# A two-block stack on one core: conv and pooling projections with 512 moving columns, part of the weight split moved to GpSimd

## The chip, the cores and the metric

The kernel runs on one core of a Trainium2 chip. The metric is the device time of one execution in microseconds. Before the change it is 1310.85 us, the median of three runs (1310.82 to 1310.9).

## The reference, cut to what matters

256 tokens of width 1024 go through two layers of a first block and one layer of a second. The change touches the first block, of which this is the part:

```
h = rms_norm(x, g_mix)
b_a, c_a, x_a, u_p, q, k, v, ga, gp, gt = split(h @ w_in)
y_a = (b_a * depthwise_conv3(c_a * x_a, conv_w)) @ w_a_out
y_p = pooled(u_p) by groups of 256 channels, windows 2, 4, 8, 16, each minus u_p,
      @ w_pool per group, * pool_scale
y_t = windowed_gqa(q, k, v, rel_bias, sink) @ w_attn_out
merged = sigmoid(ga) * y_a + sigmoid(gp) * y_p + sigmoid(gt) * y_t
x = x + merged @ w_o
h2 = rms_norm(x, g_ffn);  x = x + swiglu(h2 @ w_gu) @ w_down
```

## The kernel before, in words

Every float32 operand of a projection is held as a rounded high part and a low part (the rest), and a product is made of three matmuls: high weights by high and by low activations, and low weights by high activations. Both parts of the activations h lie beside each other in `h`.

The weights come as a stream of chunks of 128 x 2048 (`STREAM`), 1 MB each. SyncE loads them into a ring of four slots (line 640), and reloads a slot when the semaphore `wl_ready` says that its low part has been made. ScalarE makes the high part of a chunk in two halves (`split_high`, line 1571), VectorE the low part, `ring - high`, in two halves (`split_low`, line 2170); the halves are 128x1024. There are two split buffers, so the high part of a chunk waits until the chunk two before it has been used by TensorE (`BEFORE`, `NEXT`). `next_high` and `next_low`, called in the handling of a job, split the chunk two ahead.

TensorE works through a fixed list of jobs, `LAYER_JOBS`, one chunk each: v, k, four q, two kd, then four rounds of c, x, b (conv gate c, conv input x, conv gate b), then ga/wa, four u (pooling inputs), gp, wp, gt, wt, wo, and the feed-forward. A job makes 256 output columns, two groups of 128, for 256 tokens. `project` (x, b, u) puts both groups into one PSUM bank, 256 columns each, and multiplies the high weights by the two parts of h in two matmuls of 256 columns (line 788), 32 in all, then the low weights in 16 (line 794). `project_both` (q, c, gate, up) multiplies the high weights by both parts in one matmul of 512 columns (line 808), 16 in all, which leaves the main product and the cross part side by side in two banks; then the low weights, 16 of 256 columns (line 814). Its result needs ScalarE to copy the cross part out of PSUM and VectorE to add the main part. c, x and b use banks 0 and 1, 2, and 3.

Attention is laid between these jobs. After a job in `ATT_EARLY` (b0, c1, b1, c2, b2, c3, b3, ga0 and on; in layer 1 also c0) TensorE turns the probabilities of two steps ago (line 1029) and makes the scores of a step (line 1017), for which VectorE must have read the scores before (`s_read`). VectorE runs `softmax_out` of the step before at the start of such a job's handling (lines 2286 to 2290) and `softmax_in` at its end (lines 2276 to 2281); ScalarE makes the exponentials between them (line 1656).

VectorE handles the jobs in order. c: sum into `stage`. x: `stage * x` into `upad` (line 2332), then three taps of the convolution for two groups (lines 2339 and 2157). b: product with the convolution into `tmp` (line 2347), low part of the next chunk, low part of `feed`. u: the window sums (line 2359), edges, difference and the low part of `feed`.

GpSimd issues DMAs: the attention bias in four groups of eight (line 667), rows, and the 48 transfers of the second block's modulation weights (line 702), each behind a wait. It also clears a few tiles and makes one tensor_tensor, over 128x8, in the second block (line 722).

## Time and profile before

| what | value |
|---|---|
| runs | 1310.85 us median (1310.82 to 1310.9) |
| the profiled execution | 1310.87 us, its span 1309.1 us |
| TensorE (PE) busy | 1293.9 us, 99% of the span |
| VectorE (DVE) busy | 1043.4 us, 80% |
| ScalarE (ACT) busy | 715.8 us, 55% |
| GpSimd (POOL) busy | 57.1 us, 4% |
| DMA | 262.64 MB, mean 201 GB/s |

The page gives busy times as shares of the span. The chain of waits goes back from the last instruction to what released it, step by step, and says on which engine the time of the chain was spent. The groups of instructions give, for each source line, the busy time, the mean time of one in ns, and the idle time of the engine just before them with what ended it. The first layer's conv rounds run from about 50 to 118.5 us, its pooling inputs from 173.6 to 196.7 us; the second layer's conv rounds from about 520 to 596 us.

### The profile page before, as it was taken

How to read it: one execution, taken by the hardware profiler on the slowest of the kernel's cores; microseconds unless marked ns; L12 is line 12 of the kernel's file. 1: busy time of each engine (PE TensorE's matmuls, PEld its weight loads, DVE VectorE, ACT ScalarE, POOL GpSimd, SP SyncE). 2: the span in 40 equal slices, each digit the busy share in tenths (PEclk: the TensorE clock that was granted, in tenths of full speed). 3: DMA queues.
4: the chain of work that ended last, by engine and by line, in shares of the span. 5: the costliest groups of instructions: out<-in, count | busy, mean ns of one | idle time of the engine just before them, and what ended most of it. 6: DMA issues, size and time to landing. Idle time of an engine off the chain costs nothing.

```text
span 1309.1 us, 19856 instructions
## 1 busy us (share of the span) xinstructions
PE 1293.9 (99%) x7564; PEld 1122.8 (86%) x7564; DVE 1043.4 (80%) x1730; ACT 715.8 (55%) x1149; POOL 57.1 (4%) x108
## 2 busy tenths in 40 slices
PE   8999999999999999999999999999999999999998
PEld 7999898888888888998898888888879887888887
DVE  4887677877778786977687777788888898798888
ACT  5655655455454455555545464454477566655554
POOL 1111000000000000000000000000010000000000
PEclk9999999999999999999999999999999999999999
DMA  8865545764777745454446755878635515255551
GB/s 292 270 212 185 177 161 212 250 232 150 271 258 284 253 165 193 161 181 153 149 162 229 274 181 216 271 280 290 236 111 176 212 66 171 103 203 187 193 192 64
DMA packets 43000, 262.64 MB, mean 201 GB/s; under 512 B 5645, under 2 KB 6413, under 8 KB 15646
## 3 DMA queue, kind: packets, MB, share of 16 engines
q1 hardware_dynamic: 32688, 227.28, 48.9%
q0 software_dynamic: 10128, 34.06, 8.2%
q8 instruction: 60, 0.98, 0.3%
q14 instruction: 30, 0.25, 0.1%
q10 hardware_dynamic: 94, 0.07, 0.0%
HBM read 259.81 MB, written 1.58 MB: 200 GB/s over the span
## 4 chain that ended last, share of the span: by engine, by line
PE 94%; DVE 3%; ACT 1%; DMA 0%; issue 0%; SPq 0%; POOL 0%; DVEq 0%; POOLq 0%; ACTq 0%
PE psum L808 21%; PE psum L855 17%; PE psum L929 12%; PE psum L814 11%; PE psum L862 9%; PE psum L788 8%; PE psum L794 4%; PE psum L1017 1%; PE psum L1040 1%; PE psum L1203 1%; PE psum L1029 1%; PE psum L947 1%; DVE split L2164 1%; DMA ring<-stream 0%; PE psum L745 0%; PE psum L826 0%
## 5 line engine op out<-in xcount | busy, mean ns | idle before, releaser
L2164 DVE TENSOR_TENSOR split<-ring,split 128x1024 fp32r<-128x1024 f32 x406 | 479.3, 1219 | 59.7 <-ACT split L1571 58.4
L1571 ACT CAST split<-ring 128x1024 fp32r<-128x1024 f32 x405 | 405.7, 1050 | 174.8 <-PE psum L929 68.2
L808 PE MATMUL psum<-h,split 128*128 128x512 f32 x1216 | 290.0, 390 | 0.0
L808 PEld LDWEIGHTS psum<-h,split 128*128 128x128 f32 x1216 | 225.0, 188 | 44.7
L929 PE MATMUL psum<-split,feed 128*128 128x512 f32 x792 | 185.2, 390 | 0.0
L929 PEld LDWEIGHTS psum<-split,feed 128*128 128x128 f32 x792 | 146.8, 188 | 29.4 <-DVE split L2164 0.2
L814 PEld LDWEIGHTS psum<-h,split 128*128 128x128 f32 x1216 | 156.2, 191 | 6.1
L814 PE MATMUL psum<-h,split 128*128 128x256 f32 x1216 | 158.0, 283 | 0.0
L855 PE MATMUL psum<-split,h 128*128 128x512 f32 x632 | 155.8, 393 | 0.1
L855 PEld LDWEIGHTS psum<-split,h 128*128 128x128 f32 x632 | 116.3, 188 | 23.6 <-issue 0.4
L788 PE MATMUL psum<-h,split 128*128 128x256 f32 x896 | 112.2, 283 | 0.0
L788 PEld LDWEIGHTS psum<-h,split 128*128 128x128 f32 x896 | 109.7, 192 | 0.2
L1691 ACT COPY arena<-psum 128x512 f32<-128x512 f32 x40 | 23.4, 586 | 114.4 <-PE psum L814 114.4
L862 PE MATMUL psum<-split,h 128*128 128x512 f32 x316 | 81.7, 390 | 0.0
L855 PE MATMUL psum<-split,feed 128*128 128x512 f32 x304 | 74.8, 392 | 0.3 <-DVE feed L2164 0.3
L862 PEld LDWEIGHTS psum<-split,h 128*128 128x128 f32 x316 | 59.3, 188 | 12.5
L1656 ACT ACTIVATE arena<-arena,small 128x256 f32<-128x256 f32 x64 | 32.1, 502 | 69.3 <-DVE small L2281 69.3
L855 PEld LDWEIGHTS psum<-split,feed 128*128 128x128 f32 x304 | 56.0, 188 | 11.7 <-DVE feed L2164 0.6
L794 PE MATMUL psum<-h,split 128*128 128x256 f32 x448 | 58.5, 283 | 0.0
L2492 DVE SCALAR_TENSOR_TENSOR arena<-arena 128x1024 f32<-128x1024 f32 x48 | 58.5, 1218 | 0.0
L794 PEld LDWEIGHTS psum<-h,split 128*128 128x128 f32 x448 | 55.9, 192 | 0.0
L2157 DVE SCALAR_TENSOR_TENSOR arena<-arena,prm 128x255 f32<-128x255 f32 (+2 forms) x120 | 52.6, 480 | 3.8 <-ACT arena L2139 2.3
(378 smaller groups left out, 1365.0 us busy)
## 6 DMA issues: line engine op xcount, KB each, us to landing
ring<-stream SPq DMA_DIRECT2D x213, 1024.0 KB, 4.9
arena<-ada POOLq DMA_DIRECT2D x48, 512.0 KB, 5.8
arena<-bias_by_distance POOLq DMA_DIRECT2D x32, 96.0 KB, 5.2
gain<-norm_rows POOLq DMA_DIRECT2D x4, 512.0 KB, 6.0
x<-x_in SPq DMA_DIRECT2D x2, 512.0 KB, 4.1
ring<-stream SPq DMA_DIRECT2D x2, 512.0 KB, 6.9
arena<-norm_rows POOLq DMA_DIRECT2D x2, 512.0 KB, 5.7
gain<-mod_rows POOLq DMA_DIRECT2D x2, 512.0 KB, 6.0
```

What stands on the lines that cost most here:

```text
L788: pe.matmul(to[m], w[0][:, at + k, cols[m]], rhs[:, part, at + k, :], start=m == parts[0] and k + part == 0, stop=False)
L794: mm = pe.matmul(to[m], w[1][:, at + k, cols[m]], rhs[:, 0, at + k, :], start=False, stop=m == parts[-1] and k == kts - 1)
L808: pe.matmul(bank[b + m].rearrange("p (a t) -> p a t", a=2), w[0][:, k, m * P:(m + 1) * P], h[:, :, k, :], start=k == 0, stop=False)
L814: mm = pe.matmul(bank[b + m][:, T:2 * T], w[1][:, k, m * P:(m + 1) * P], h[:, 0, k, :], start=False, stop=k == KT - 1)
L855: pe.matmul(bank[banks[i]], lhs[:, part, k0 + k, at], w[0][:, k, :], start=k0 + k + part == 0, stop=False)
L862: mm = pe.matmul(bank[banks[i]], lhs[:, 0, k0 + k, at], w[1][:, k, :], start=False, stop=k0 + k == KT - 1)
L929: mm = pe.matmul(bank[4 + 2 * i + n], feed[:, part, place, at], w[which][:, k, cols], start=j + k + part + which == 0, stop=last and j == ...
L1571: act.copy(split_of(x)[:, 0, n], ring[:, AT[x] % RING, n]).then_inc(wh_ready, 1)
L1656: act.activation(S1[:, i % 2, hh, :], S1[:, i % 2, hh, :], ACT.Exp, scale=-1.0, bias=nm[:, i % 2, hh:hh + 1], accum_out=rs[:, i % 2, hh:hh ...
L2157: return dve.scalar_tensor_tensor(out_, a, s, b, op0, op1)
L2164: return dve.tensor_tensor(out_, value, high.bitcast(F32), ALU.subtract)
L2492: dve.scalar_tensor_tensor(w, w, 0.5, c_row, ALU.mult, ALU.mult, accum_out=mod_l[:, a:a + 1]) \
```

## The change

x, b and u jobs are made by `project_both` as well: 16 matmuls of 512 columns in place of 32 of 256. Each of these jobs then leaves a cross part. ScalarE copies it (into `tmp` for x, `stage` for b, `padded` for u) and VectorE adds the main part before it goes on as before. The three conv jobs use two pairs of banks in turn (0 and 1, 2 and 3), and so do the u jobs; a job waits until the sum of the job two before it is made (`wide_summed`). For 14 chunks a layer (b0, c, x and b of rounds 1 to 3, u0 to u3) GpSimd makes the second half of the low part; VectorE makes the first, and waits before the first half of the following chunk until GpSimd's is counted, so that `wl_ready` goes up in order. In GpSimd's queue three of these stand between bias groups 1 and 2 (the wait for x1's job is gone), seven between groups 2 and 3, four behind the loads for the second block, and in layer 1 all 14 ahead of the modulation transfer 24.

The diff, cut to its core:

```diff
+POOL_LOWS = ([("b", 0)] + [(n, j) for j in (1, 2, 3) for n in ("c", "x", "b")] + [("u", j) for j in range(4)])
...
+        def summed(l, name, j):
+            return wide_summed, l * 16 + (12 + j if name == "u" else 3 * j + "cxb".index(name)) + 1
+
+        def conv_bank(name, j):
+            return ({"c": 0, "x": 2, "b": 0}, {"c": 2, "x": 0, "b": 2})[j % 2][name]
...
+            def second_low(x):
+                n = slice(CHUNK // 2, CHUNK)
+                pool.wait_ge(wh_ready, AT[x] * 2 + 2)
+                pool.wait_ge(wl_ready, AT[x] * 2 + 1)
+                pool.tensor_tensor(split_of(x)[:, 1, n], ring[:, AT[x] % RING, n], split_of(x)[:, 0, n].bitcast(F32), ALU.subtract) \
+                    .then_inc(wl_ready, 1)
...
             bias_group(1)
-            pool.wait_ge(job_done, JOB["x", 1])
+            for x_ in POOL_LOWS[0:3]:
+                second_low((0, *x_))
             bias_group(2)
+            for x_ in POOL_LOWS[3:10]:
+                second_low((0, *x_))
             pool.wait_ge(job_done, JOB["b", 3])
             bias_group(3)
...
+            for x_ in POOL_LOWS[10:]:
+                second_low((0, *x_))
...
+                if a == ADA_L:
+                    for x_ in POOL_LOWS:
+                        second_low((1, *x_))
...
TensorE's waits and jobs:
+                    elif (name, j) == ("x", 0):
+                        pe.wait_ge(*release(("kd", 1), l))
+                    elif name == "x":
+                        pe.wait_ge(*summed(l, "b", j - 1))
+                    elif name == "b":
+                        pe.wait_ge(*summed(l, "c", j))
+                    elif name == "u" and j < 2:
+                        pe.wait_ge(*release((("ga", 3), ("wa", 3))[j], l))
+                    elif name == "u":
+                        pe.wait_ge(*summed(l, "u", j - 2))
...
-                    elif name in ("x", "b"):
-                        mm = project(CONV_BANK[name], c, h)
+                    elif name in ("c", "x", "b"):
+                        mm = project_both(conv_bank(name, j), c)
...
+                    elif name == "u":
+                        mm = project_both(2 * (j % 2), c)
...
ScalarE:
+                    elif name == "x":
+                        act.wait_ge(job_done, l * NJOBS + k + 1)
+                        if j >= 1:
+                            act.wait_ge(yin_ready, l * 4 + j)
+                        act.copy(tmp, cross_part(conv_bank(name, j))).then_inc(wide_cross, 1)
+                    elif name == "b":
+                        act.wait_ge(job_done, l * NJOBS + k + 1)
+                        act.wait_ge(dve_evac, l * len(DVE_JOBS) + dve_count(("x", j)))
+                        act.copy(stage, cross_part(conv_bank(name, j))).then_inc(wide_cross, 1)
...
-                        act.copy(padded[:, :, PADW:PADW + T], src).then_inc(act_evac, 1)
+                        act.copy(padded[:, :, PADW:PADW + T], cross_part(2 * (j % 2))).then_inc(act_evac, 1)
...
VectorE:
             def split_low(x, half_=None):
                 for half in range(2) if half_ is None else (half_,):
+                    if half and x[0] < L and x[1:] in POOL_LOWS:
+                        continue
+                    before = STREAM[AT[x] - 1]
+                    if half == 0 and before[0] < L and before[1:] in POOL_LOWS:
+                        dve.wait_ge(wl_ready, AT[x] * 2)
...
+                        dve.wait_ge(*summed(l, "c", j))
+                        dve.wait_ge(wide_cross, l * 8 + 2 * j + 1)
+                        dve.tensor_tensor(tmp, main_part(conv_bank(name, j)), tmp, ALU.add).then_inc(wide_summed, 1)
+                        dve.wait_ge(*summed(l, "x", j))
+                        dve.tensor_tensor(upad[:, :, 1:1 + T], tmp, stage, ALU.mult).then_inc(dve_evac, 1)
...
+                        dve.wait_ge(wide_cross, l * 8 + 2 * j + 2)
+                        dve.tensor_tensor(stage, main_part(conv_bank(name, j)), stage, ALU.add).then_inc(wide_summed, 1)
+                        dve.wait_ge(*summed(l, "b", j))
+                        dve.tensor_tensor(tmp, stage, y1, ALU.mult).then_inc(dve_evac, 1)
...
+                        u_ = padded[:, :, PADW:PADW + T]
+                        dve.tensor_tensor(u_, main_part(2 * (j % 2)), u_, ALU.add).then_inc(wide_summed, 1)
+                        dve.wait_ge(*summed(l, "u", j))
```

## Rows read from the trace of the kernel before

**Rows 1.** The page: busy time by engine; the granted clock; the chain by engine.

```profile
PE 1293.9 (99%) x7564; PEld 1122.8 (86%) x7564; DVE 1043.4 (80%) x1730; ACT 715.8 (55%) x1149; POOL 57.1 (4%) x108
PEclk9999999999999999999999999999999999999999
PE 94%; DVE 3%; ACT 1%; DMA 0%; issue 0%; SPq 0%; POOL 0%; DVEq 0%; POOLq 0%; ACTq 0%
```

**Rows 2.** Waits of PE, the longest in total: total us, times, longest us.

```profile
PE psum L826 <- DVE h L2164: 1.8, 3, 0.9
```

**Rows 3.** Busy time by stretch: a conv round of layer 0, the u jobs.

```profile
core 0: us, PE busy (x) PEld busy (x) DVE busy (x) ACT busy (x) POOL busy (x), PEclk, DMA share, GB/s
81.50:100.40 18.90, 18.90 (x146) 18.23 (x145) 16.50 (x40) 10.21 (x21) 0.00 (x0) 1.00 0.47 167
173.60:196.70 23.10, 23.10 (x194) 23.07 (x193) 18.73 (x33) 11.30 (x14) 0.00 (x0) 1.00 0.47 170
```

**Rows 4.** Timeline of PE, conv jobs of both layers: start us, duration us.

```profile
69.10 4.00 PE L788 MATMUL psum<-h,split 128*128 128x256 f32 x32
72.94 2.08 PE L794 MATMUL psum<-h,split 128*128 128x256 f32 x16
...
557.20 3.83 PE L808 MATMUL psum<-h,split 128*128 128x512 f32 x16
560.87 2.08 PE L814 MATMUL psum<-h,split 128*128 128x256 f32 x16
```

**Rows 5.** Groups by line of PE: busy us, mean ns | idle before.

```profile
L808 PE MATMUL psum<-h,split 128*128 128x512 f32 x1216 | 290.0, 390 | 0.0
L788 PE MATMUL psum<-h,split 128*128 128x256 f32 x896 | 112.2, 283 | 0.0
```

**Rows 6.** Groups by line: the copy of ACT, the sum of DVE.

```profile
L1731 ACT COPY arena<-psum 128x512 f32<-128x512 f32 x8 | 4.7, 587 | 17.0 <-PE psum L794 17.0
L2328 DVE TENSOR_TENSOR arena<-psum,arena 128x512 f32<-128x512 f32 x8 | 5.5, 685 | 0.4 <-ACT arena L1729 0.4
```

**Rows 7.** Groups by line of POOL: all its tensor work.

```profile
L709 POOL MEMSET arena<- 128x1024 f32 x3 | 2.7, 954 | 13.6 <-PE psum L862 13.6
L722 POOL TENSOR_TENSOR arena<-arena 128x8 f32<-128x8 f32 x1 | 1.7, 1673 | 88.4 <-DVE arena L2850 88.4
L719 POOL MEMSET arena<- 128x8 f32 x1 | 0.1, 124 | 0.0
```

**Rows 8.** DVE beside POOL's memsets: timeline, and the cast line's min/median/max.

```profile
961.36 1.51 POOL L706 MEMSET arena<- 128x512 f32 x4 [22.63 <-DVE x L2157]
962.58 0.57 DVE L2572 CAST h<-arena 128x512 fp32r<-128x512 f32 x1
...
976.50 2.74 POOL L709 MEMSET arena<- 128x1024 f32 x3 [13.62 <-PE psum L862]
976.52 2.36 DVE L2164 TENSOR_TENSOR split<-ring,split 128x1024 fp32r<-128x1024 f32 x2
...
L2572 DVE CAST h<-arena x8: 420/427/574, 959.5 to 1125.5; 128x512 fp32r<-128x512 f32 x8
```

**Rows 9.** Timeline behind a b job of layer 0, PE and DVE.

```profile
97.18 2.36 DVE L2164 TENSOR_TENSOR split<-ring,split 128x1024 fp32r<-128x1024 f32 x2
100.44 3.83 PE L808 MATMUL psum<-h,split 128*128 128x512 f32 x16
104.26 0.48 DVE L2276 CUSTOM_DVE_ANT_0 arena<-psum,arena,minus_sinks 128x256 f32<-128x256 f32 x1
106.19 0.16 DVE L2286 TENSOR_TENSOR small<-small 128x2 f32<-128x2 f32 x1 [1.25 <-ACT small L1658]
106.38 0.72 PE L1017 MATMUL psum<-k_pair,q_first 128*128 128x256 f32 x4
112.89 0.69 DVE L2332 TENSOR_TENSOR arena<-psum,arena 128x512 f32<-128x512 f32 x1 [1.72 <-PE psum L794]
```

**Rows 10.** Timeline of POOL: a group of bias DMAs.

```profile
69.08 4.15 POOL L667 DMA_DIRECT2D arena<-bias_by_distance  x8 [19.09 <-PE psum L814]
```

More of the change, by code:

```diff
@@ L465, in bass_stack_kernel @@
         feed_high = sem("feed_high")
-        c_summed = sem("c_summed")
+        wide_summed = sem("wide_summed")
+        wide_cross = sem("wide_cross")
         ao_split = sem("ao_split")
@@ L1057, in _ @@
                         if (name, j) == ("ga", 0):
-                            pe.wait_ge(c_summed, l * 4 + 4)
+                            pe.wait_ge(*summed(l, "x", 3))
+                        elif name == "gp" and j % 2 == 0:
+                            pe.wait_ge(*summed(l, "u", 2 + j // 2))
                         elif j % 2 == 0:
@@ L1074, in _ @@
                         else:
-                            pe.wait_ge(c_summed, l * 4 + j)
-                    elif name in ("x", "b"):
-                        pe.wait_ge(*release((name, j - 1) if j else ("kd", CONV_BANK[name] - 2), l))
+                            pe.wait_ge(*summed(l, "x", j - 1))
+                    elif (name, j) == ("x", 0):
[8 more added lines that the diff above has]
+                        pe.wait_ge(*summed(l, "u", j - 2))
                     elif k >= 4 and name != "wo" and LAYER_JOBS[k - 4][0] != "wo":
@@ L1727, in _ @@
                         if j >= 1:
-                            act.wait_ge(dve_evac, l * len(DVE_JOBS) + dve_count(("x", j - 1)))
-                        act.copy(stage, cross_part(CONV_BANK[name])).then_inc(act_evac, 1)
+                            act.wait_ge(dve_evac, l * len(DVE_JOBS) + dve_count(("b", j - 1)))
+                        act.copy(stage, cross_part(conv_bank(name, j))).then_inc(act_evac, 1)
+                    elif name == "x":
[7 more added lines that the diff above has]
+                        act.copy(stage, cross_part(conv_bank(name, j))).then_inc(wide_cross, 1)
                     elif name == "u":
-                        act.copy(padded[:, :, PADW:PADW + T], src).then_inc(act_evac, 1)
+                        act.copy(padded[:, :, PADW:PADW + T], cross_part(2 * (j % 2))).then_inc(act_evac, 1)
                     if name == "wo" and j == 1:
@@ L2327, in _ @@
                         dve.wait_ge(act_evac, l * len(ACT_JOBS) + act_count(("c", j)))
-                        dve.tensor_tensor(stage, main_part(CONV_BANK[name]), stage, ALU.add).then_inc(c_summed, 1)
+                        dve.tensor_tensor(stage, main_part(conv_bank(name, j)), stage, ALU.add).then_inc(wide_summed, 1)
                     if name == "x":
-                        dve.wait_ge(c_summed, l * 4 + j + 1)
-                        dve.tensor_tensor(upad[:, :, 1:1 + T], halves(CONV_BANK[name]), stage, ALU.mult).then_inc(dve_evac, 1)
+                        dve.wait_ge(*summed(l, "c", j))
[3 more added lines that the diff above has]
+                        dve.tensor_tensor(upad[:, :, 1:1 + T], tmp, stage, ALU.mult).then_inc(dve_evac, 1)
                         dve.wait_ge(dve_evac, l * len(DVE_JOBS) + dve_count(("x", j)))
@@ L2346, in _ @@
                             dve.wait_ge(yin_ready, l * 4 + j)
-                        dve.tensor_tensor(tmp, halves(CONV_BANK[name]), y1, ALU.mult).then_inc(dve_evac, 1)
+                        dve.wait_ge(wide_cross, l * 8 + 2 * j + 2)
+                        dve.tensor_tensor(stage, main_part(conv_bank(name, j)), stage, ALU.add).then_inc(wide_summed, 1)
+                        dve.wait_ge(*summed(l, "b", j))
+                        dve.tensor_tensor(tmp, stage, y1, ALU.mult).then_inc(dve_evac, 1)
                         next_low((l, name, j))
```

4 lines of the change are left out of this document (removed).

## The prediction, made before the run

> **What bounds the kernel now.** I read the page first. TensorE is busy 1293.9 of 1309.1 us and carries 94% of the chain of waits, and the granted clock is full, level 2.4 GHz, in every slice; VectorE is busy 80%, ScalarE 55%, GpSimd 4% [rows 1]. Then TensorE's own waits: the longest in total is 1.8 us, three times, and belongs to none of the conv or pooling-input jobs [rows 2]. So TensorE's issue sets the time, and a change can gain only by fewer or cheaper matmuls. It can lose much more, by making TensorE wait. The second question is therefore how near VectorE is to the bound in the stretch that changes. In one round of three conv jobs (c, x, b) TensorE needs 18.9 us and VectorE is busy 16.5; in the four pooling-input jobs it is 18.7 of 23.1 [rows 3]. A round leaves VectorE only 2.4 us.
>
> The profiled execution took 1310.87 us, 1.77 beyond its span of 1309.1; the median is 1310.85, so the sum needs no correction.
>
> **The gain: wide matmuls.** Per job, 32 matmuls of 256 columns (high weights by both parts of h) become 16 of 512; the 16 low ones stay. In the timeline 32 narrow ones take 3.84 us up to the first low one (69.10 to 72.94), 16 wide ones 3.67 (557.20 to 560.87) [rows 4]: 0.17 us a job. The whole-run groups give 32 x 112.2/896 = 4.01 against 16 x 290.0/1216 = 3.82, or 0.19 [rows 5]. I take 0.175. x, b and u are 12 jobs a layer, 24 in all: 24 x 0.175 = 4.2 us, bounds 4.1 and 4.6. TensorE is the bound here, so all of it counts if nobody else becomes late. The weight loads halve too, which hides behind the columns.
>
> **ScalarE.** x and b now each need a copy of the cross part, 0.586 us; u had its copy already, of the same size [rows 6]. That is 8 x 0.59 = 4.7 us a layer on an engine busy about 10 us of a round's 18.9 [rows 3]. I cost its busy time at nothing, but not its order: x's copy stands behind the previous step's exponentials, and VectorE's sum for x waits for it.
>
> **VectorE, added and removed.** Added: 12 sums a layer from PSUM, 0.69 us each [rows 6], 2 to a round: +1.4. Removed: the second low half of 14 chunks, 1.18 us each (two take 2.36) [rows 8], 3 to a round: -3.5. So VectorE's own round falls from 16.5 to 14.4, under TensorE's new 18.9 - 2 x 0.175 = 18.55. If this were all, the change would be a clean gain.
>
> **GpSimd's halves: their length.** No row has a GpSimd subtraction of this size. From below: its memset of 128x1024 takes 0.95 us, one of 128x8 0.12, so one stream of 1024 costs 0.83 above a fixed 0.12; the instruction must also read two tiles. From above: its one tensor_tensor, a power over 128x8, took 1.67 us; with three streams of 0.83 behind that, 4.2 [rows 7]. Two input streams taken in turn give 1.8, all three in turn 2.6: I take 2.2. The Trainium skill, GPSIMD Engine Reference, section 3.1, measures 4497 ns for 2048 elements, by which this would be an estimate of 2.25 us; no run shows it yet.
>
> Is TensorE late for them? Each is needed when the job reaches its fifth low matmul, 3.67 + 0.48 = 4.15 us into the job, and the first half was ready before the job began in this trace's rounds (low of c's chunk 97.2 to 99.5, c begins 100.44) [rows 9]. VectorE's next first half also waits for it, about 3.3 us later. At 2.2 us neither waits; from about 5 us TensorE would.
>
> **GpSimd beside VectorE.** This decides the sign. Before, GpSimd never reads tiles while VectorE does. What the trace has: two lows of VectorE beside three memsets took 2.36 us, not slowed at all; but a VectorE cast beside a memset took 574 ns where its median is 427 [rows 8]. So the two engines do hinder each other in some pairings, and the new one, both reading two SBUF tiles, is not among those shown. Bounds: nothing, or the whole 2.2 us of each half during which every VectorE instruction with two SBUF inputs stands still. I take the whole for those instructions: reading is what both do most here, and the one pairing that was hindered shows that access is not free. The Trainium skill, SBUF — State Buffer, section "Who interferes with whom", states this outright: a VectorE instruction with two SBUF inputs contends with a GpSimd one that reads SBUF, not with one that only writes, and whoever comes second blocks for the whole instruction. Its second half agrees with the undisturbed lows of [rows 8]; the first no row shows.
>
> Now the round, at full taking of turns. Three halves are 3 x 2.2 = 6.6 us. Beside two of them VectorE can do the score instructions, which read PSUM, two of 0.48 us a step [rows 9]: 1.9 overlap, 4.7 left. 14.4 + 4.7 = 19.1. Two idle times don't go away: softmax_out waits 1.25 us for ScalarE's exponentials where steps follow each other [rows 9], and x's sum now waits for ScalarE's copy behind the exponentials (copy, 0.59, and part of the 1.7 us that VectorE idled for TensorE there before): I count 1.0. Together 21.35 against 18.55: VectorE is 2.8 us a round late. With a hold of h in place of 2.2 this is 3h - 3.8.
>
> Where it lands, by the round whose c job begins at 100.44: softmax_out, sum, product, first low and feed low follow. GpSimd's half (started by the first low of the c chunk) holds 2.2 of it, the sum adds 0.69, the missing half gives back 1.18. The second score instruction began at 104.26 and TensorE asked for it at 106.38 [rows 9], so a first delay of 1.7 is covered. In the next rounds it is TensorE's scores (the wait on s_read) that are late, and behind them x's job; the chunk lows of c come 1 us late too. Attention steps run in every round, so nothing recovers before ga. The rounds concerned are about three a layer (b of round 0 to b of round 3): 6 x 2.8 = 16.8, less the 1.7 of cover in each layer, 3.4: 13.4 us lost. In the pooling stage VectorE's round gives 4 x 0.69 more and four halves elsewhere; it has 4.4 us free, and four gate jobs with little VectorE work follow: at most 0.5 a layer, counted 0.
>
> Sum: -4.2 + 13.4 = +9.2, 1310.85 + 9.2 = 1320.
>
> **Other moved things, cost nothing.** Bank waits: x, b, c now wait for the sum two jobs back, 1.3 to 2 us after that job, with a job of 5.6 between. Later low halves delay a ring slot's reload by 2 us: a chunk is loaded about three jobs (17 us) ahead. GpSimd's queue: the 8 bias DMAs of 4.15 us each group [rows 10] now stand behind or between the lows; the next low is needed some 8 us later, and the heads they bring only at step 8. In layer 1 the lows stand ahead of an ada transfer that waited for the last pooling job anyway.
>
> **Rivals.**
> A, no hindrance: GpSimd works truly beside VectorE. For it: undisturbed lows beside memsets. Against: those only write. VectorE keeps 14.4 + 2.3 of waits = 16.7 under 18.55, TensorE never waits: 1310.85 - 4.2 = 1306.7.
> B, partial: the halves fall into VectorE's idle time more than I count, or are shorter. A hold of 1.7 us loses 3 x 1.7 - 3.8 = 1.3 a round, 7.8 in six, less 3.4 of cover is 4.4, which eats the gain: 1311.
> C, a GpSimd half takes 4.2 us or more, the bound from above: 3 x 4.2 - 3.8 = 8.8 a round, 52.8 in six, less 3.4 and the gain of 4.2 is +45: 1356, and from about 5 us TensorE waits for the halves themselves.
> The other side of the forecast is A; it decides from the point where the hold is under 1.7 us, for then the round's loss no longer pays for the gain.
>
> **Chances.** Forecast 0.52 (own range 1314.5 to 1333: holds of 1.9 us, 11.4 - 3.4 - 4.2 = +3.8, to 2.6, 24.0 - 3.4 - 4.2 = +16.4, and 6 more if the cover is less and the pooling stage pays too), A 0.35, B 0.09, C 0.04. A measurement tells 0.2%, 2.6 us, from no change. Faster: A and a hold so small that gain remains, 0.36. Same 0.10. Slower 0.54. The range goes from under A, 1305.8, to 1333.
>
> **What would show it.** Gain right: the groups of 256-column high matmuls of x, b, u gone, 384 more wide ones, 3.66 us from first wide to first low. Hold right: during each GpSimd subtraction no VectorE instruction with two SBUF inputs is under way (or it is stretched to its end), TensorE waits for VectorE before the score matmuls and the c jobs, and a round takes over 20 us. A right: rounds of 18.5 us and VectorE idle over 3 us in each. Wrong altogether: loss in the pooling stage, or waits on bank sums.

## The result and the profile after

The changed kernel takes 1333.86 us (median; 1332.51 to 1334.18) beside 1310.88 us for the kernel before on the same chip: a ratio of 1.0173, 95% interval 1.016 to 1.0186, or 23.0 us slower. The forecast was 1320.0 (+9.2) and the range ended at 1333.0: the sign was right, the size was not.

The page after, for [rows 1]: busy time by engine, the granted clock in 40 slices, the chain of waits by engine.

```profile
PE 1298.3 (97%) x7180; PEld 1106.4 (83%) x7180; DVE 1065.7 (80%) x1726; ACT 722.9 (54%) x1165; POOL 127.5 (10%) x136
PEclk9999999999999999999999999999999999999999
PE 79%; DVE 14%; issue 3%; ACT 3%; DMA 0%; SPq 0%; POOL 0%; DVEq 0%; ACTq 0%; POOLq 0%
```

TensorE has 384 matmuls fewer and is busy 4.4 us more in a span of 1332.0, and the chain now lies with VectorE for 14% of the time (3% before). TensorE's own waits after, for [rows 2] (total us, times, longest us):

```profile
PE psum L1040 <- DVE small L2323: 9.9, 7, 2.4
PE psum L1052 <- ACT gain L1700: 3.0, 2, 1.8
PE psum L1052 <- ACT arena L1700: 3.0, 3, 1.3
...
PE psum L837 <- POOL split L682: 1.5, 3, 0.6
```

L1040 is the score matmul (L1017 before) and L2323 VectorE's score instruction (L2276): seven times TensorE stood before a score because the last one had not been read. L1052 (L1029) turns the probabilities. The first row is the largest, and stood in no such place before. L1700 is ScalarE's copy of the turned probabilities out of PSUM. The wait for GpSimd's own result, the last row, is small.

The matmul groups, for [rows 5] (busy us, mean ns | idle before; L831 is the wide line, L811 what is left of the narrow one):

```profile
L831 PE MATMUL psum<-h,split 128*128 128x512 f32 x1600 | 384.0, 392 | 0.2 <-DVE k_pair L2206 0.2
L811 PE MATMUL psum<-h,split 128*128 128x256 f32 x128 | 16.2, 284 | 0.0
```

1216 wide and 896 narrow ones took 402.2 us; 1600 and 128 take 400.2. That is 2.0 less, not the 24 x 0.19 = 4.6 of the means of [rows 5]. Most of the other 2.6 went to a slower clock, below.

A round, for [rows 3] (stretch: its us, then busy time by engine, granted clock, DMA share, GB/s): from the start of c2 to the start of c3, in layer 0 and in layer 1.

```profile
83.81:105.28 21.47, 19.23 (x115) 16.66 (x113) 18.01 (x33) 11.17 (x23) 7.49 (x3) 1.00 0.43 147
569.00:592.37 23.37, 20.81 (x114) 17.90 (x113) 19.81 (x37) 11.19 (x23) 7.46 (x3) 0.93 0.39 135
```

The round takes 21.47 us where it took 18.90, and three subtractions of GpSimd fill 7.49 of it, 2.5 each. The second round has a granted clock of 0.93.

Now the hold itself. The timeline of VectorE, GpSimd and TensorE in layer 1 (start us, duration us):

```profile
549.65 2.39 POOL L682 TENSOR_TENSOR split<-ring,split 128x1024 fp32r<-128x1024 f32 x1 [7.16 <-DVE split L2206]
549.81 2.65 DVE L2336 TENSOR_SCALAR arena<-arena,small 128x256 f32<-128x256 f32 x2
...
554.84 0.68 DVE L2206 TENSOR_TENSOR feed<-arena,feed 128x512 fp32r<-128x512 f32 x1
555.07 2.69 POOL L682 TENSOR_TENSOR split<-ring,split 128x1024 fp32r<-128x1024 f32 x1 [3.02 <-DVE split L2206]
555.44 0.48 DVE L2323 CUSTOM_DVE_ANT_0 arena<-psum,arena,minus_sinks 128x256 f32<-128x256 f32 x1
...
555.84 0.48 DVE L2323 CUSTOM_DVE_ANT_0 arena<-psum,arena,minus_sinks 128x256 f32<-128x256 f32 x1
...
556.37 1.40 DVE L2328 TENSOR_TENSOR small<-sinks,small 128x2 f32<-128x2 f32 x1
556.39 0.74 PE L1040 MATMUL psum<-k_pair,q_first 128*128 128x256 f32 x4 [2.06 <-DVE small L2323]
```

Read the ends. GpSimd's first subtraction ends at 552.04; two small tensor_scalars, begun 0.16 us after it and of 0.35 us each when nothing is beside them, end at 552.46, one of them stretched over the whole subtraction. The second subtraction ends at 557.76, and a tensor_tensor over 128x2, an instruction of 0.16 us, ends at 557.77. Between them the score instructions, one input of which lies in PSUM, run beside it at their usual 0.48. One line's shortest, median and longest time says the same of all executions:

```profile
L2336 DVE TENSOR_SCALAR arena<-arena,small x64: 336/352/2385, 73.0 to 712.4; 128x256 f32<-128x256 f32 x64
...
L2328 DVE TENSOR_TENSOR small<-sinks,small x32: 160/162/2074, 71.2 to 710.3; 128x2 f32<-128x2 f32 x32
...
L2323 DVE CUSTOM_DVE_ANT_0 arena<-psum,arena,minus_sinks x64: 470/479/485, 70.2 to 709.8; 128x256 f32<-128x256 f32 x64
```

The first two have the same medians as undisturbed ones and maxima of a whole GpSimd instruction; the third, with its PSUM input, never moves. The Trainium skill, SBUF — State Buffer, section "Who interferes with whom", says that of the two engines the second to issue blocks for the whole of the other's instruction, and that a VectorE instruction with at most one SBUF input, outside the two-port modes, is not concerned; these rows agree, at 2.39 and 2.69 us a time.

And the clock. TensorE after two waits in a row (timeline), and the granted clock of the first 2 us behind them:

```profile
576.87 0.63 PE L1052 MATMUL psum<-cst,arena 128*128 128x128 f32 x4 [1.27 <-ACT arena L1700]
578.19 1.01 PE L1040 MATMUL psum<-k_pair,q_first 128*128 128x256 f32 x4 [0.69 <-DVE small L2323]
578.99 5.15 PE L831 MATMUL psum<-h,split 128*128 128x512 f32 x16
```

```profile
579.00:581.00 2.00, 2.00 (x6) 1.61 (x6) 0.72 (x2) 1.41 (x6) 0.54 (x1) 0.50 0.34 53
```

The clock is at 0.50, the 1.2 GHz level, and 16 wide matmuls take 5.15 us where they take 3.81 at 2.4 GHz. It happened three times (16 in 4.84 from 115.50, 5.15 here, 5.39 from 622.64), each time behind two waits with 0.63 us of work between them (1.27 and 0.69, twice; 0.42 and 1.83); the score matmuls before them took 0.3 and 0.5 longer in two of them. Together 1.0 + 1.3 + 1.6 + 0.8 = 4.7 us. Not every such place does it: behind the 2.06 us of 556.39 the next 16 took 3.81, and so they did at 93.24, behind 1.27 and 0.69 again.

Where the 22.9 us of the span arise can be read from the start of the score matmuls by stage, each kernel less the kernel before the change. (The numbers are differences of timeline starts; the experiments' columns are used below.)

| behind job | before, us | after | e1 | e7 | e2 | e9 | e8 | e12 |
|---|---|---|---|---|---|---|---|---|
| layer 0 c1 | 68.62 | +2.56 | +1.65 | +2.67 | +1.40 | +0.46 | +0.36 | -0.21 |
| layer 0 c2 | 87.47 | +5.20 | +4.04 | +4.95 | +1.82 | +1.67 | -0.04 | -0.60 |
| layer 0 ga0 | 127.27 | +9.26 | +5.69 | +6.35 | +1.85 | +2.16 | -0.75 | -1.32 |
| layer 0 gp0 | 204.56 | +8.48 | +4.89 | +5.58 | +1.85 | +1.37 | -1.55 | -2.12 |
| layer 1 c0 | 525.74 | +10.26 | +5.92 | +6.45 | +1.87 | +1.40 | -1.57 | -2.11 |
| layer 1 b3 | 596.55 | +16.44 | +8.38 | +8.75 | +1.87 | +2.24 | -3.06 | -3.59 |
| layer 1 ga1 | 609.32 | +20.72 | +10.10 | +10.47 | +1.88 | +2.25 | -3.05 | -3.58 |
| layer 1 gp0 | 680.21 | +19.92 | +9.30 | +9.67 | +1.87 | +1.45 | -3.85 | -4.38 |
| span | 1309.1 | +22.9 | +11.5 | +11.7 | +3.2 | +2.4 | -3.6 | -4.5 |

The columns do not start at zero: at the first score matmul (62.59) they already stand between -0.2 and +0.7 (after 0.0, e1 +0.3, e7 +0.7, e2 +0.2, e9 +0.5, e8 +0.4, e12 -0.2), so they are read by their steps. In the column "after" the loss comes in both layers' conv rounds and the first gates behind them, 0.8 comes back in each pooling stage, and 1.8 and 3.0 are lost behind gp0.

### The profile page after: what moved, and what is told of

Its sections match the earlier page's. It is cut to its first block, busy times and chain, and to the rows that moved or that the text cites. A ratio compares the mean times of both kernels' runs of the same rounds, so it can differ in the third digit from the quotient of the medians.

```text
span 1332.0 us, 19192 instructions
## 1 busy us (share of the span) xinstructions
PE 1298.3 (97%) x7180; PEld 1106.4 (83%) x7180; DVE 1065.7 (80%) x1726; ACT 722.9 (54%) x1165; POOL 127.5 (10%) x136
## 4 chain that ended last, share of the span: by engine, by line
PE 79%; DVE 14%; issue 3%; ACT 3%; DMA 0%; SPq 0%; POOL 0%; DVEq 0%; ACTq 0%; POOLq 0%
PE psum L831 21%; PE psum L878 16%; PE psum L952 12%; PE psum L837 11%; PE psum L885 8%; DVE split L2206 3%; DVE arena L2415 1%; DVE small L2328 1%; DVE arena L2199 1%; PE psum L1236 1%; PE psum L811 1%; DVE arena L2323 1%; PE psum L1063 1%; PE psum L970 1%; DVE feed L2206 1%
## 5 line engine op out<-in xcount | busy, mean ns | idle before, releaser
L2206 DVE TENSOR_TENSOR split<-ring,split 128x1024 fp32r<-128x1024 f32 x378 | 447.7, 1220 | 53.3 <-ACT split L1604 52.0
L831 PE MATMUL psum<-h,split 128*128 128x512 f32 x1600 | 384.0, 392 | 0.2 <-DVE k_pair L2206 0.2
L831 PEld LDWEIGHTS psum<-h,split 128*128 128x128 f32 x1600 | 297.6, 189 | 59.6 <-DVE k_pair L2206 0.4
L837 PEld LDWEIGHTS psum<-h,split 128*128 128x128 f32 x1600 | 205.6, 191 | 10.1 <-POOL split L682 2.1
L837 PE MATMUL psum<-h,split 128*128 128x256 f32 x1600 | 208.6, 283 | 1.5 <-POOL split L682 1.5
L682 POOL TENSOR_TENSOR split<-ring,split 128x1024 fp32r<-128x1024 f32 x28 | 70.2, 2506 | 261.8 <-DVE split L2206 254.6
L1724 ACT COPY arena<-psum 128x512 f32<-128x512 f32 x40 | 23.5, 586 | 114.0 <-PE psum L837 114.0
L725 POOL DMA_DIRECT2D arena<-ada x48 | 25.5, 531 | 448.6 <-DVE arena L2548 444.4
L2505 DVE TENSOR_TENSOR arena<-psum,arena 128x512 f32<-128x512 f32 x20 | 13.8, 690 | 36.4 <-ACT arena L1724 36.4
L2171 ACT COPY arena<-psum 128x512 f32<-128x512 f32 x22 | 12.9, 585 | 51.2 <-PE psum L837 46.9
```

Of the source, the lines that this page charges most:

```text
L682: pool.tensor_tensor(split_of(x)[:, 1, n], ring[:, AT[x] % RING, n], split_of(x)[:, 0, n].bitcast(F32), ALU.subtract) \
L725: pool.dma_start(ada_ring[:, a % 2, :], ada[a]).then_inc(ada_loaded[a % 2], 16)
L831: pe.matmul(bank[b + m].rearrange("p (a t) -> p a t", a=2), w[0][:, k, m * P:(m + 1) * P], h[:, :, k, :], start=k == 0, stop=False)
L837: mm = pe.matmul(bank[b + m][:, T:2 * T], w[1][:, k, m * P:(m + 1) * P], h[:, 0, k, :], start=False, stop=k == KT - 1)
L2206: return dve.tensor_tensor(out_, value, high.bitcast(F32), ALU.subtract)
```

## The experiments

The theory: GpSimd's reading halves hold VectorE's SBUF instructions, and TensorE waits for the scores. Rivals: the wide jobs themselves are what costs; GpSimd's place in the hand-over of low parts costs, not its reading.

**The two parts alone.** e1 is the changed kernel without GpSimd's halves, e2 the kernel before with them.

```diff
e1, against the changed kernel:
-POOL_LOWS = ([("b", 0)] + [(n, j) for j in (1, 2, 3) for n in ("c", "x", "b")] + [("u", j) for j in range(4)])
+POOL_LOWS = []
...
             bias_group(1)
+            pool.wait_ge(job_done, JOB["x", 1])
e2, against the kernel before:
+POOL_LOWS = ([("b", 0)] + [(n, j) for j in (1, 2, 3) for n in ("c", "x", "b")] + [("u", j) for j in range(4)])
...
(second_low, its places in GpSimd's queue, and split_low's two conditions, as in the change)
```

> The changed kernel with no chunk given to GpSimd: x, b and u stay wide, VectorE makes every low half. Theory 1 (taking of turns between GpSimd's and VectorE's instructions costs the time): VectorE's round is 16.5 + 1.4 = 17.9 us busy, with 1.25 us of waiting for exponentials and 1.0 for x's copy 20.15 against TensorE's 18.55; 1.6 us a round late, 9.6 in six, less 3.4 of cover and the gain of 4.2: about 1313 us, at any rate 15 us or more under the changed kernel's 1333.9. Rival 1 (the added sums and copies of the wide jobs overload VectorE and ScalarE, GpSimd only helps): slower than the changed kernel, over 1336 us. Rival 2 (the second half is only late, and the ordered waits on it stall VectorE): 1307 to 1313 us, as theory 1.

> The kernel before with GpSimd making the second low half of the same 14 chunks a layer; x, b and u stay narrow. Theory 1: a GpSimd half holds VectorE's tensor_scalars and two-input instructions for about 2.5 us; the round is 16.5 - 3.5 + 7.5 - 1.9 + 1.25 = 19.85 us against 18.9, 5.7 us in six rounds less the cover of 3.4: about 1313 us, up to 1318 where TensorE's stalls lower its clock. The tensor_scalar pair behind x's first low half takes over 2 us, as in the changed kernel. Rival 1: VectorE is relieved of 28 x 1.18 = 33 us and nothing is added, so 1310.9 or less. Rival 2: within 3 us of the kernel before, with waits of VectorE for GpSimd in the trace.

Measured: e1 1322.13 us (ratio 1.0084, 1.0069 to 1.01; before 1311.05), e2 1314.08 (1.0023, 1.0013 to 1.0032). So the wide jobs alone lose 11.1 us, the halves alone 3.0, and both together 23.0: more than the sum by 8.9. Taken alone, the wide jobs, which remove TensorE work, cost the more. For e1 no range that was expected held: the theory had 1313, and 1336 or more was the rival's; e2 came out as expected. The waits of e1 and its timeline behind a b job show why the wide jobs lose:

```profile
PE psum L1041 <- DVE small L2324: 9.2, 7, 1.9
```

```profile
107.30 0.68 DVE L2399 TENSOR_TENSOR arena<-psum,arena 128x512 f32<-128x512 f32 x1
108.02 0.69 DVE L2401 TENSOR_TENSOR arena<-arena 128x512 f32<-128x512 f32 x1
108.63 2.35 DVE L2207 TENSOR_TENSOR split<-ring,split 128x1024 fp32r<-128x1024 f32 x2
...
110.90 0.68 DVE L2207 TENSOR_TENSOR feed<-arena,feed 128x512 fp32r<-128x512 f32 x1
...
111.50 0.48 DVE L2324 CUSTOM_DVE_ANT_0 arena<-psum,arena,minus_sinks 128x256 f32<-128x256 f32 x1
...
111.90 0.48 DVE L2324 CUSTOM_DVE_ANT_0 arena<-psum,arena,minus_sinks 128x256 f32<-128x256 f32 x1
...
112.44 0.74 PE L1041 MATMUL psum<-k_pair,q_first 128*128 128x256 f32 x4 [0.54 <-DVE small L2324]
```

VectorE's order for a b job is: sum, product, two lows of the next chunk, the low of `feed`, and only then the score instructions. The wide job puts the sum, 0.7 us, and ScalarE's copy ahead of all that, and VectorE arrives at the scores after TensorE has asked for them. No engine is overloaded in this: product, lows and the low of `feed`, 3.7 us that TensorE does not yet wait for, stand ahead of 0.9 us on which it depends. e1 has one slow stretch of the clock too: behind waits of 0.41 and 1.82 us, 16 wide matmuls took 5.42 us.

**Only some wide jobs.** e4 is the kernel before with u alone made wide, e5 has u, x (and c in its new banks) wide, b narrow; neither has GpSimd's halves.

```diff
e4, against the kernel before:
+                    elif name == "u":
+                        mm = project_both(2 * (j % 2), c)
...
+                        dve.tensor_tensor(u_, main_part(2 * (j % 2)), u_, ALU.add).then_inc(u_summed, 1)
e5, against e1:
-                    elif name in ("c", "x", "b"):
+                    elif name in ("c", "x"):
                         mm = project_both(conv_bank(name, j), c)
+                    elif name == "b":
+                        mm = project(conv_bank(name, j), c, h)
...
```

> The kernel before with only the u jobs wide, conv jobs narrow, nothing for GpSimd. Gain of 0.175 to 0.2 us a job on TensorE, 8 jobs: 1.4 to 1.6 us. VectorE gets 8 more sums of 0.69 us. Theory 1, with its own sum of the pooling stage (4.4 us free): all of the gain stays, 1309.3 us. Rival 1: VectorE in the pooling stage is late for gate pooling's lows and scores (the changed kernel lost 1.8 and 3 us there), so 1311 to 1315 us.

> No GpSimd halves; c, x and u wide, b narrow. Theory 1a, formed after the first four runs: each sum added to a conv round makes VectorE's score instructions late, and they release TensorE's next scores; with x and b wide (1322.1 us) a round has two such sums, here one, and b's job, behind which the covers are thinnest, has none. x's sum lies in a job without scores. Expected: conv rounds near 18.7 us, loss of 1 to 4 us a layer mostly from x's sum pushing the lows and the b handling, the gate pooling loss of the wide-u run (1.6 us net) unchanged: 1312 to 1316 us. Rival 1a (the loss comes from the two-bank-pair scheme and its waits for sums, the same for c, x): stays near 1322 us.

Measured: e4 1312.62 us (1.0012, 1.0003 to 1.0021), e5 1317.17 (1.0046, 1.0031 to 1.0062; before 1311.33). u alone gains 0.8 us in each pooling stage and loses more behind it, 1.0 us in layer 0 and 2.1 in layer 1; the expectation's own theory had all of the gain staying, and its rival is what came. VectorE comes out of the stage later, and in layer 0 the scores behind gp0 are asked for before they are read (timeline of e4).

```profile
207.86 2.34 DVE L2173 TENSOR_TENSOR split<-ring,split 128x1024 fp32r<-128x1024 f32 x2
...
210.53 0.48 DVE L2285 CUSTOM_DVE_ANT_0 arena<-psum,arena,minus_sinks 128x256 f32<-128x256 f32 x1
...
211.07 0.73 PE L1018 MATMUL psum<-k_pair,q_last 128*128 128x256 f32 x4 [0.76 <-DVE small L2285]
```

Again two lows stand ahead of the scores. In layer 1 the exponentials that follow the late scores begin at 689.21, and ScalarE's copy of the turned probabilities comes behind them and other work at 693.14; TensorE waits 1.79 us for it. Each against its own before, e4 loses 1.6, e5 5.8 (1.2 over the range expected) and e1 11.1: x adds 4.3 and b 5.2, 1.6 of which is e1's slow stretch of the clock, so both share the loss.

**Scores first.** If the order is the cause, moving the score instructions ahead of the lows must turn the loss into the gain. e8 does this to e1, e10 to the kernel before, e9 to the changed kernel.

```diff
+                def scores_in(k):
+                    if ATT_LAYER[l].get(k, ATT_STEPS) < UNITS1:
+                        softmax_in(ATT_LAYER[l][k])
...
                         dve.tensor_tensor(tmp, stage, y1, ALU.mult).then_inc(dve_evac, 1)
+                        scores_in(k)
                         next_low((l, name, j))
...
+                    if name != "b":
+                        scores_in(k)
...
-                    if ATT_LAYER[l].get(k, ATT_STEPS) <= UNITS1:
-                        i = ATT_LAYER[l][k]
-                        if i < UNITS1:
-                            softmax_in(i)
```

> The kernel with x, b and u wide and no GpSimd halves (1322.1 us), with one change of order on VectorE: softmax_in, which releases TensorE's next scores, runs before the job's low halves (and feed low) instead of after them. Theory 1a (TensorE is late for scores, not for weights): the scores come 2.3 to 3 us earlier, the lows 1.1 us later, which have over 3 us of cover; TensorE's waits vanish and the gain shows: 1307 to 1310 us. Rival 3 (VectorE simply has too much to do, whatever the order: 20.15 us a round against 18.55): the waits move from the scores to the lows, 1318 us or more.

> The kernel before with the same change of order alone. TensorE waits nowhere in these stages before, so nothing can be gained there: 1310.8 to 1311.2 us by theory 1a and by rival 3. If the order itself helps anywhere (gate pooling's or the value step's waits), up to 1 us less.

> The changed kernel with the same change of order: softmax_in before the first low half. Now GpSimd's half starts after the score instructions and no longer runs beside them, but beside the feed low and the next softmax_out. Theory 1a with the hold: scores are no longer late, but VectorE's round is 14.4 + 7.5 + 1.25 = 23.1 us less whatever idle time covers, against 18.55: still late, TensorE waits for lows; 1318 to 1330 us. If the holds cost only through the scores' lateness (theory 1b): 1307 to 1312 us.

Measured: e8 1307.32 us (0.997, 0.9957 to 0.9982), e10 1311.19 (0.9999, 0.999 to 1.0008), e9 1313.29 (1.0015, 1.0006 to 1.0024), before 1311.33. e8 and e10 came out as expected; e9 fell between its two ranges, 5 us under the lower end of the theory that had holds making VectorE late whatever the order. Each against its own runs of before: the order gives nothing where the scores were in time (e10, -0.1), 15.1 us to the wide jobs (from +11.1 to -4.0) and 21.0 to the changed kernel (from +23.0 to +2.0). e8 is faster than both kernels, and its 4.0 us are the forecast's gain of 4.2. Its timeline at the place that e1 showed above:

```profile
101.62 0.68 DVE L2403 TENSOR_TENSOR arena<-psum,arena 128x512 f32<-128x512 f32 x1
102.34 0.69 DVE L2405 TENSOR_TENSOR arena<-arena 128x512 f32<-128x512 f32 x1
102.95 0.48 DVE L2324 CUSTOM_DVE_ANT_0 arena<-psum,arena,minus_sinks 128x256 f32<-128x256 f32 x1
...
103.95 2.36 DVE L2207 TENSOR_TENSOR split<-ring,split 128x1024 fp32r<-128x1024 f32 x2
...
105.98 0.72 PE L1041 MATMUL psum<-k_pair,q_first 128*128 128x256 f32 x4
```

The scores are read 2 us before TensorE wants the bank. The round before this one, in e8:

```profile
81.51:100.05 18.54, 18.54 (x114) 16.56 (x113) 17.13 (x37) 11.30 (x23) 0.00 (x0) 1.00 0.49 171
```

18.54 us against the forecast's 18.55, with VectorE at 17.13 and both low halves on it. What e9 has left over e8, 6.0 us, is what the halves cost once the order is right: no score wait is left in it, but TensorE still waits four times, 0.94 to 1.27 us, for ScalarE's copy of the turned probabilities in the conv rounds, which e8 does not show.

**Writing without reading.** e3 is the changed kernel with each subtraction replaced by three memsets (1024, 1024 and 512 columns); the second low halves are then zero. e12 is the same with the scores first.

```diff
-                pool.tensor_tensor(split_of(x)[:, 1, n], ring[:, AT[x] % RING, n], split_of(x)[:, 0, n].bitcast(F32), ALU.subtract) \
-                    .then_inc(wl_ready, 1)
+                m = 3 * POOL_DONE.setdefault(x, len(POOL_DONE))
+                pool.memset(split_of(x)[:, 1, n].bitcast(F32), 0.0).then_inc(pool_step, 1)
+                pool.wait_ge(pool_step, m + 1)
+                pool.memset(split_of(x)[:, 1, n].bitcast(F32), 0.0).then_inc(pool_step, 1)
+                pool.wait_ge(pool_step, m + 2)
+                pool.memset(split_of(x)[:, 1, slice(CHUNK // 2, 3 * CHUNK // 4)].bitcast(F32), 0.0).then_inc(pool_step, 1)
+                pool.wait_ge(pool_step, m + 3)
+                pool.sem_inc(wl_ready, 1)
```

> The changed kernel, but GpSimd only writes: in place of each subtraction it clears the same half with two memsets of 128x1024 and one of 128x512, about 2.4 us in sum, with the same waits before and the same count after; it reads no tile (the second low halves are zero, so part of the product is left out). Theory 1 in the form that the reads collide: VectorE's tensor_tensor is not held, a tensor_scalar perhaps is by up to 2 us a round; rounds near 18.6 us, 1307 to 1312 us. Rival 2 (waits and order, not the access to SBUF): the same length stands in the same place, so 1330 us or more. Rival 1 (the wide jobs' own sums and copies): also 1330 or more.

> The changed kernel with the early score instructions, and each GpSimd subtraction replaced by memsets of the same length that read nothing (the second low halves are zero). Theory (only the reading holds VectorE's tensor_tensors): 1307.3, as without GpSimd's halves, bounds 1306.5 and 1308.5, since the memsets still hold tensor_scalars of the taps for about 1 us. Rival (what costs is GpSimd's place in the handing over of ring slots and low parts, or its length): as the changed kernel with the early order, 1313.3.

Measured: e3 1311.09 us (1.0, 0.999 to 1.0009), e12 1306.68 (0.9967, 0.9955 to 0.998; before 1310.87). GpSimd is as long in the way (0.96 + 0.96 + 0.54 us) and in the same place of every hand-over, but it does not read, and the 23.0 us go (6.2 from e9 to e12, each against its own before). So the halves' cost is the reading, not the hand-over. That zeros stand in the second low halves does not make TensorE's matmuls shorter: the wide and the low groups take 381.7 and 208.0 us in e9, 381.8 and 207.8 in e12. e3 also shows what e1's loss hangs on: with the second halves off VectorE the wide jobs lose 0.0 in place of 11.1 in the old order, as one low of 1.2 us less stands ahead of the scores, but they do not gain their 4.2 either; that takes the scores first. A memset is not free of hold (timeline of e3):

```profile
82.72 0.96 POOL L685 MEMSET split<- 128x1024 f32 x1 [5.34 <-DVE split L2214]
82.91 1.97 DVE L2344 TENSOR_SCALAR arena<-arena,small 128x256 f32<-128x256 f32 x2
83.74 0.98 POOL L687 MEMSET split<- 128x1024 f32 x1
```

Each of the two tensor_scalars, 0.35 us by itself, ends 0.15 us behind a memset. That is the cast's 574 ns of [rows 8] again: tensor_scalar and cast are held by a write, the lows of [rows 8], with two inputs, are not. (The same section of the Trainium skill puts this down to the two-port modes that copy, cast and tensor_scalar can enter; the rows show who is held, not the mode.)

**Half the length.** In e7 GpSimd takes the last 512 columns, VectorE the 512 before.

```diff
-                n = slice(CHUNK // 2, CHUNK)
+                n = slice(3 * CHUNK // 4, CHUNK)
...
+                pool.wait_ge(quarter, 1 + [(l_, *y) for l_ in range(L) for y in POOL_LOWS].index(x))
...
+                        n = slice(CHUNK // 2, 3 * CHUNK // 4)
...
+                        low(split_of(x)[:, 1, n], ring[:, AT[x] % RING, n], split_of(x)[:, 0, n]).then_inc(quarter, 1)
```

> The changed kernel, but GpSimd makes only the last 512 columns of each of the 14 second halves (128x512, an estimate of 1.3 us from 2.5 for 1024), and VectorE the 512 before them (0.6 us). Theory (loss goes with the time that GpSimd reads): a hold of 1.3 us and 0.6 us of work in place of a hold of 2.5: 0.6 us less a chunk, of the 11.8 us that the halves cost over the wide jobs alone a third to a half goes: 1327 to 1330, and less if TensorE's clock falls in fewer stretches. Rival (each half costs a fixed hand-over, whatever its length): 1334 or more, as VectorE's work is 0.6 us more a chunk.

Measured: 1322.52 us (1.0088, 1.0071 to 1.0105), 11.7 over before, where e1 has 11.1. The expectation was right in its direction and too small: the length halves (1393 ns in the mean) and of the 11.9 us that the halves cost over e1 0.6 is left, or about 2 if e1's slow stretch of the clock (1.6 us; e7 has none) is taken out. Not a third to a half goes, but over four fifths.

```profile
L684 POOL TENSOR_TENSOR split<-ring,split 128x512 fp32r<-128x512 f32 x28 | 39.0, 1393 | 280.7 <-DVE split L2208 280.7
```

A hold of 1.4 us with 0.6 of own work stands for 1.2 of removed work and falls in part beside PSUM instructions; it comes out nearly even. At 2.5 us it does not. So the loss is no constant per half. Against e1, the halves give back 11.1 us without reading (e3), cost 0.6 at 1.4 us and 11.9 at 2.5 us; VectorE's own work differs between these three, so they do not show whether there is a threshold.

**Only where there is room.** e11 is e8 with GpSimd's halves for u0 to u3 alone.

```diff
-POOL_LOWS = []
+POOL_LOWS = [("u", j) for j in range(4)]
```

> The wide jobs with the early score instructions (1307.3 us), and GpSimd's halves for the four pooling-input chunks of each layer only. Theory (the halves hold VectorE, and that costs only where VectorE has no room): the pooling stage leaves VectorE 4.4 of 23.1 us, four halves hold at most 4 x 2.5 of which much falls beside PSUM work and idle time; but the changed kernel lost 1.8 us a layer in the gates behind this stage. If that loss comes from these halves, 1307.3 + 2 x 1.8 = 1311; if it was left over from the conv rounds, 1307.3 to 1308. I expect 1309. Rival (a GpSimd half is harmless in itself and the losses came from the conv order): 1307.3 or less.

Measured: 1307.98 us (0.9978, 0.9968 to 0.9987), 2.9 under its own before where e8 is 4.0 under, with overlapping intervals. The 1311 that would have put the loss behind gp0 on these halves did not come. In the profiled execution the 1.0 us that e11 lies over e8 arises in one place, gp0 of layer 1, where TensorE waits 0.40 us in the middle of the job for a low of VectorE; the changed kernel and e9 have the same wait there. So of the 1.8 and 3.0 us behind gp0, 1.0 and 2.1 are the late scores that e4 has too, and most of the rest goes with the halves.

## Why the prediction was right or wrong

**Bound and gain: right.** TensorE's issue was the bound, and no wait of TensorE for a bank's sum shows in the conv rounds. e8 gains 0.35 to 0.4 us in each conv round and 0.8 in each pooling stage, 4.0 in all against 4.2; e12 4.2.

**ScalarE: busy time right, order nearly.** Its copies cost nothing by themselves: e8 has them all, and TensorE waits for ScalarE nowhere in its conv rounds. Of TensorE's waits on L1700 after, 6.0 us, 3.4 are left in e9, where no score is late, and none in e12: those go with the held instructions of VectorE, not with its order alone.

**GpSimd's length: too small, without effect on the time held.** 2.38 to 2.73 us, 2506 ns in the mean, against 2.2; the Trainium skill, GPSIMD Engine Reference, section 3.1, gave an estimate of 2.25 by half of 2048 elements. Inside the bounds of 1.8 and 2.6 for the mean. By the prediction's own formula 3h - 3.8 a round would lose 3.7 in place of 2.8, and the sum would be +14.6. But the longer halves did not hold VectorE longer than was forecast. Of the 7.5 us of GpSimd in layer 0's round from c2, these instructions lost 4.8 (two tensor_scalars 2.64 where they take 0.62, the 128x2 one 1.41 and 1.72 where it takes 0.16); the prediction had 4.7 of 6.6.

```profile
86.11 2.64 DVE L2336 TENSOR_SCALAR arena<-arena,small 128x256 f32<-128x256 f32 x2
...
92.65 1.41 DVE L2328 TENSOR_TENSOR small<-sinks,small 128x2 f32<-128x2 f32 x1
...
98.91 1.72 DVE L2328 TENSOR_TENSOR small<-sinks,small 128x2 f32<-128x2 f32 x1
```

**Not late for the halves themselves: nearly right.** TensorE waited for GpSimd's half three times behind the fourth low matmul, 0.28, 0.62 and 0.60 us, where the prediction had no wait below 5 us. It counted on a first half that is ready before the job begins; in these rounds VectorE was late with it, and in e9 the waits are gone.

**The hold: right in kind.** Taken whole, with instructions that have a PSUM input free; the rows of the 128x2 instruction and e3 show it. It fell on other instructions than the forecast named: over the whole kernel the tensor_scalars of L2336, with one tile as input, take 30.0 us where e1 has 19.8, and the 128x2 ones of L2328 25.1 where e1 has 5.2; the chunk lows with their two SBUF inputs lost nothing (1220 ns in the mean in both), as they run ahead of GpSimd's half. Rival A (no hindrance, 1306.7) is out. Its number is what e12 measures, but that needs both: no reading and the scores first; in the order of the change, without the reading (e3), it is 1311.1. Rival B's hold of 1.7 and rival C's half of 4.2 us did not occur.

**The step that failed: "So VectorE's own round falls from 16.5 to 14.4, under TensorE's new 18.9 - 2 x 0.175 = 18.55. If this were all, the change would be a clean gain."** It compares busy sums. e3 is the run nearest to it: the sums are there, the second halves are off VectorE and nobody reads beside it, and the kernel is at 0.0 where a clean gain is -4.2; with the scores first (e12) the 4.2 are there. With the halves left on VectorE, still 17 of 18.5 us busy, the old order makes it +11.1 (e1) and the new one -4.0 (e8). The score instructions stood at the end of VectorE's list for the job, and the new sum and the wait for ScalarE's copy went ahead of them in attention jobs. The prediction looked at this cover once, at the place of [rows 9] (read at 104.74, asked for at 106.38), set 2.2 + 0.69 - 1.18 = 1.7 against it and went on with busy sums. The round that it judged by is the one with the most cover: of the places behind c1, c2 and c3 in layer 0 it is the last. The other two, behind c1 and c2, have 0.72 and 0.57 us before the change:

```profile
67.42 0.48 DVE L2276 CUSTOM_DVE_ANT_0 arena<-psum,arena,minus_sinks 128x256 f32<-128x256 f32 x1
...
68.62 0.64 PE L1017 MATMUL psum<-k_pair,q_first 128*128 128x256 f32 x4
...
86.42 0.48 DVE L2276 CUSTOM_DVE_ANT_0 arena<-psum,arena,minus_sinks 128x256 f32<-128x256 f32 x1
...
87.47 0.72 PE L1017 MATMUL psum<-k_pair,q_first 128*128 128x256 f32 x4
```

A sum of 0.69 us is as much as these two have. Behind c1 TensorE waited 1.15 us in e1 and 2.42 after, behind c3 0.54 and 0.69.

**What the busy sum could not tell: the same hold at three prices.** The time for which VectorE is held is its busy time less that of the kernel without halves, and plus the 31.6 us of lows that GpSimd takes over: 37.9 us after, 34.0 in e9, 35.3 in e2. (By the same count the memsets held it for 7.4 us in e3 and 12.1 in e12.) Against the writing kernels it costs 23.0 us in the changed kernel, 4.7 of it by the clock, and 6.2 with the scores first (e9 against e12); e2 as a whole loses 3.0. What is held is nearly the same; where the awaited instructions stand, and what is put ahead of them, decides.

**Rounds and cover: the round right by luck, the rest too mild.** The round from c2 in layer 0 took 21.47 us against 18.54 in e8, 2.9 more, and 2.8 was forecast. But VectorE was busy for only 18.0 us of it, less than 18.55; TensorE waited for an order and not for a full engine. The conv rounds and first gates together lost 10.8 us in layer 0 and 12.0 in layer 1, gain taken out (9.26 + 1.5, and 20.72 - 10.26 + 1.5), where the prediction had 6.7 in each. The cover of 1.7 a layer did not show, and layer 1's first gates lost with the rounds (a score wait of 1.83 us, and the clock behind it).

**Pooling stage counted 0: right for the stage, wrong behind it.** It gave back its 0.8 in both layers, as VectorE has room there; but 1.8 and 3.0 us went behind gp0. The prediction counted on gate jobs "with little VectorE work"; the scores there come late by the order, too (e4: 1.0 and 2.1), and e11 leaves about 1 us in layer 1 for the halves.

**Not in the sum at all: the clock.** 4.7 us at 1.2 GHz, read from the after trace, contained in the losses above. A stall of TensorE cost more than its length. No run here isolates it; of the other kernels only e1 has such a stretch, one.

The balance of the span: 22.8 lost in conv rounds and first gates, 4.8 behind gp0, less 4.6 gained, is 23.0 of 22.9 measured. Beside the forecast's +9.2 that is 13.8 more: 4.8 behind gp0, counted 0; 4.7 by the clock, not in the sum; 4.7 more in rounds and first gates, 3.4 of it the cover; less 0.4 of gain. By parts: the wide jobs in the old order +11.1, the halves on top +11.9. The second number is close to the 13.4 that the prediction had for them, the first was to be -4.2; with the price of the halves between 6 and 23 us by what they are set against, the nearness of 11.9 is luck. Of the 11.9, 3.1 is the clock (4.7 after against 1.6 in e1), if its stretches cost what their matmuls show. What stays open: how the other 8.8 divides between the hold itself, which with the scores first costs 6.0 (e9 over e8), and its meeting with scores that are late already; and what decides whether a wait brings the clock down.

## What to carry to other kernels

Before engines' busy sums are compared, find for every instruction that another engine waits on when it is done and when it is asked for, at each of its places and not at one; whatever is put ahead of it in its queue is charged against that margin in each repetition. When work on the bounding engine gets shorter at the price of a little work elsewhere, first move those awaited instructions ahead of what nobody waits for: here that was worth 15.1 us with wide jobs and nothing without. A GpSimd instruction that reads SBUF is to be kept short, or put beside VectorE's PSUM work: 1.4 us at a time cost 0.6 to 2 us in all here, 2.5 us at a time 11.9 in the same places, and 6.0 with the awaited instructions first.

## What the runs showed of the hardware that was not expected

- GpSimd reading two SBUF tiles (128x1024, 2.38 to 2.73 us) held even a VectorE tensor_tensor over 128x2 (0.16 us) to its end, up to 2.07 us, and a tensor_scalar of 0.35 us up to 2.39 us; score instructions, with one input in PSUM, stayed at 0.48 us.
- GpSimd memsets of 0.96 us, which read nothing, held a tensor_scalar (0.35 us became 1.12) but no low with two SBUF inputs.
- GpSimd's subtraction took 2.39 us where it began first (549.65) and 2.69 where it began inside a running low of `feed` (555.07, the low until 555.52), as if it were held in its turn until that ended and finished its own reading in the rest; 1.29 to 1.60 us for 512 columns. That the difference is a hold is an inference from such places, not tested.
- TensorE's clock fell to 1.2 GHz in three places after and one in e1, each time behind two waits with 0.63 us of work between them (1.27 and 0.69 twice, 0.42 and 1.83, 0.41 and 1.82), and 16 matmuls of 512 columns then took 4.84 to 5.42 us for 3.82. It did not fall behind another 1.27 and 0.69, behind 0.85 and 1.29 in e7, or behind single waits of 2.42 and 2.06 us.
